# Reordering the two mixing branches of a transformer block: later stick-breaking sums and outputs, decays prepared one pair ahead, output norms moved beside the next pair

## The reference, cut to what matters

```python
h = rms_norm(x, mix_norm_w)
proj = einsum('bsd,de->bse', h, w_in)            # all projections of both branches
# branch 1: stick-breaking attention, 8 heads of 128
q, k = rms_norm(q, sb_q_norm_w), rms_norm(k, sb_k_norm_w)
z = q k^T / sqrt(128);  log_1mb = log_sigmoid(-z) below the diagonal
a = exp(log_sigmoid(z) + suffix_sum(log_1mb));   o_sb = a v
# branch 2: gated delta rule, 8 heads of 128, chunks
gq, gk, gv = silu(conv4(...));  gq, gk = l2_normalize(gq), l2_normalize(gk)
decay = exp(gc_i - gc_j) below the diagonal      # gc: running sum of the log decay
L = strict_lower(k_beta k^T * decay);  T = inverse(I + L)
v_corr = T v_beta;  k_cum = T (k_beta exp(gc));  attn = lower(q k^T * decay)
for chunk in chunks:                             # the recurrence over the state
    v_new = v_corr - k_cum state;  o = q exp(gc) state + attn v_new
    state = state * exp(g_last) + (k exp(g_last - gc))^T v_new
o_gdn = rms_norm(o, gdn_out_norm_w) * silu(z)
x = x + (sigmoid(gate_sb) * (o_sb @ W1) + sigmoid(gate_gdn) * (o_gdn @ W2)) @ w_out
```

## Time and profile before

| | |
|---|---|
| median of 3 runs | 3158.27 us (3157.06 to 3158.77) |
| the profiled execution, its own time | 3154.85 us |
| its span, first to last instruction | 3153.1 us |
| PE busy | 2820.9 us, 89% of the span |
| DVE busy | 1959.8 us, 62% |
| ACT busy | 1168.5 us, 37% |
| POOL busy | 529.7 us, 17% |
| mean granted TensorE clock | 0.95 of full |

### The profile page before, as it was taken

How to read it: one execution, slowest core, us unless ns; L and a number is a source line. 1 busy time by engine, 2 the same in 40 slices (tenths; PEclk the granted TensorE clock), 3 DMA queues, 4 the chain that set the end, 5 groups by cost and what they waited for, 6 DMA issues and landing times.

```text
span 3153.1 us, 36626 instructions
## 1 busy us (share of the span) xinstructions
PE 2820.9 (89%) x14045; PEld 2383.0 (76%) x14045; DVE 1959.8 (62%) x3668; ACT 1168.5 (37%) x1688; POOL 529.7 (17%) x392
## 2 busy tenths in 40 slices
PE   7987798898998799998898799999999878899997
PEld 5666586687776688888898688888888536688876
DVE  3233365465564478989999578787886495354434
ACT  4433433432322333333788222222223344232222
POOL 0111101101000176766211011101110011000000
PEclk9998898899999899998999899999999888999999
DMA  3111111000554256666788788888885200122221
GB/s 135 47 47 47 73 41 41 27 14 28 187 216 165 93 206 249 246 241 235 272 309 321 280 300 293 292 297 295 297 291 183 75 0 28 67 103 91 96 91 40
DMA packets 141357, 501.17 MB, mean 159 GB/s; under 512 B 13400, under 2 KB 66944, under 8 KB 111744
## 3 DMA queue, kind: packets, MB, share of 16 engines
q1 hardware_dynamic: 122752, 364.60, 32.6%
q0 software_dynamic: 18432, 134.23, 10.9%
HBM read 450.53 MB, written 48.25 MB: 158 GB/s over the span
## 4 chain that ended last, share of the span: by engine, by line
PE 63%; DVE 19%; DMA 6%; ACT 5%; issue 3%; POOL 3%; SPq 0%; DVEq 0%; POOLq 0%; ACTq 0%
PE bank L236 17%; PE bank L237 17%; PE bank L238 17%; DMA gs<-in_uv_dram,idx 4%; DVE HA L1823 2%; DVE bank L1491 2%; DVE gs L1478 2%; PE bank L938 1%; PE bank L2395 1%; PE bank L633 1%; PE bank L954 1%; PE bank L948 1%; DVE xn L1289 1%; DVE HO L1820 1%; PE bank L644 1%
## 5 line engine op out<-in xcount | busy, mean ns | idle before, releaser
L236 PE MATMUL bank<-HH,uhl 128*128 128x384 f32 x1024 | 358.8, 350 | 38.5 <-POOL uhl L1413 38.4
L237 PE MATMUL bank<-HL,uhl 128*128 128x384 f32 x1024 | 353.5, 345 | 0.0
L238 PE MATMUL bank<-HH,uhl 128*128 128x384 f32 x1024 | 353.3, 345 | 0.0
L236 PE MATMUL bank<-vhl,awhl 128*128 128x512 f32 x768 | 299.7, 390 | 21.3 <-DVE awhl L2017 21.3
L238 PE MATMUL bank<-vhl,awhl 128*128 128x512 f32 x768 | 299.6, 390 | 0.0
L237 PE MATMUL bank<-vhl,awhl 128*128 128x512 f32 x768 | 299.5, 390 | 0.0
L1467 POOL DMA_INDIRECT gs<-in_uv_dram,idx x128 | 161.4, 1261 | 762.6 <-DVE x L1491 505.3
L1980 ACT ACTIVATE vhl<-vraw 128x1024 fp32r<-128x1024 f32 x128 | 135.8, 1061 | 413.2 <-PE bank L238 272.2
L236 PEld LDWEIGHTS bank<-HH,uhl 128*128 128x128 f32 x1024 | 199.2, 195 | 45.3 <-issue 35.8
L1413 POOL TENSOR_TENSOR uhl<-ur,uhl 128x1024 fp32r<-128x1024 f32 x66 | 159.9, 2429 | 430.3 <-ACT uhl L1407 430.0
L236 PE MATMUL bank<-HH,whl 128*128 128x512 f32 x512 | 212.8, 416 | 18.7 <-DVE whl L232 13.1
(11 more groups left out here) (406 smaller groups left out, 6299.6 us busy)
## 6 DMA issues: line engine op xcount, KB each, us to landing
ur<-in_peer_u_dram SPq DMA_DIRECT2D x128, 512.0 KB
vraw<-in_peer_v_dram SPq DMA_DIRECT2D x128, 512.0 KB, 3.7
w_raw<-in_w_in_dram SPq DMA_DIRECT2D x36, 1024.0 KB, 6.1
xn<-in_ada_rows_dram SPq DMA_DIRECT2D x48, 512.0 KB, 4.7
g_scratch<-stg SPq DMA_DIRECT2D x12, 2048.0 KB, 11.3
gti<-g_scratch SPq DMA_DIRECT2D x16, 1536.0 KB, 9.8
wf_raw<-in_f_w_in_dram SPq DMA_DIRECT2D x22, 1024.0 KB, 4.8
act_scratch<-ag SPq DMA_DIRECT2D x96, 192.0 KB
```

Of the source, the lines that this page charges most:

```text
L236: e.matmul(out, l[0], r[0], start=start, stop=False)
L237: e.matmul(out, l[0], r[1], start=False, stop=False)
L238: return e.matmul(out, l[1], r[0], start=False, stop=stop)
```

## The change

The change writes the lists in another order, and moves buffers so that this is allowed. No matmul and no element-wise product is dropped, except that a [128 x 4] exponential (EGL) is added for each head. Its parts:

- **Start.** Mean square and root are taken row block by row block (`rows_done`). The identity alone is fetched for the transposes, then weights 0, then the other constants. The first weights are split between the third and the fourth tile of HH and HL. PE runs the first two projection steps tile by tile (`pe_sb_first`, `proj_T2`), each as soon as its HL tile is there.
- **Stick-breaking.** The sums move from segment 3 to 4, the exponential to 5, the output matmuls to segment 0 of the next pair (segment 6 for the last). The output copy and its DMA go along.
- **Delta-rule decays.** `pe_decay`, `act_decay`, `dve_decay`, `pool_decay`, `act_decay_exp`, `dve_decay_beta` now run for pair g + 1 within segments 15 to 21 of pair g, and for the first pair within segments 7 to 9 of the last stick-breaking pair.
- **Projection norms.** The squares of the second two tiles get buffers of their own, so all four go together in segments 10 to 12.
- **Output norms.** `pe_gdn_norm`, `act_gdn_norm`, `dve_gdn_norm` run in segments 0 and 1 of the next pair. The output now waits in the XT buffer, so POOL must wait for it before it writes the next XT.
- Explicit loads of the logarithm table on ACT at the head of each pair and in each norm are gone.

```diff
@@ act_norm1, dve_norm1
-        root_x(e, A, V, 0, NT)
-        high_x(e, T, A, R1, lambda kt: vcol("mix_norm_w", kt))
+            if tb:
+                root_x(e, A, V, tb - 1, 1)
+        high_x(e, T, A, R1, lambda kt: vcol("mix_norm_w", kt), range(3))
+        split_hi(e, W, 0)
+        high_x(e, T, A, R1, lambda kt: vcol("mix_norm_w", kt), range(3, KT))
...
@@ pe_sb
+    def pe_sb_first(e):
+        e.wait_ge(*W.low(0).of(0))
+        outs = [R2.take("proj", 0, f)[:, :] for f in range(2)]
...
+        for f, i in enumerate(proj_T2(e, outs, W, 0, wait)):
+            i.then_inc(*T.up("proj", 0, f))
+        W.used(0, T, "proj", 0, 1)
+        pe_sb_norm(e, 0, 0)
...
@@ pe_sb_head: sums along the row
-        if seg == 3:
+        if seg == 4:
@@ pe_sb: outputs
+                if seg == 0 and pair:
+                    for hh in range(2):
+                        pe_sb_out(e, pair - 1, hh)
                 pe_sb_head(e, pair, 0, seg)
                 pe_sb_head(e, pair, 1, seg)
+                if pair == 3 and seg == 6:
+                    for hh in range(2):
+                        pe_sb_out(e, 3, hh)
...
@@ dve_gdn
-            for seg in range(25):
+            for seg in range(24):
                 dve_gdn_head(e, 2 * g, seg)
                 dve_gdn_head(e, 2 * g + 1, seg)
+                if g and seg == 1:
+                    for f in range(2):
+                        dve_gdn_norm(e, 2 * g - 2 + f)
                 if g < 3:
                     dve_gdn_proj(e, R3, g + 1, seg)
+                    for f in range(2):
+                        if seg == 17:
+                            dve_decay(e, R3, 2 * g + 2 + f)
+                        if seg == 21:
+                            dve_decay_beta(e, 2 * g + 2 + f)
...
@@ pe_gdn
+                if g and seg == 0:
+                    for f in range(2):
+                        pe_gdn_norm(e, 2 * g - 2 + f)
                 if g < 3:
                     pe_gdn_proj(e, R3, g + 1, seg)
+                    if seg == 15:
+                        for f in range(2):
+                            pe_decay(e, R3, 2 * g + 2 + f)
@@ pool_gdn_head, seg 1
             e.wait_ge(*A.of("lt", h))
+            if h >= 2:
+                e.wait_ge(*V.of("onw", h - 2))
             e.tensor_tensor(B["XT"][:, :, :], B["LT"][:, :, :], cb("neg1T"), ALU.mult)
```

More of the change, by code:

```diff
@@ L304, in turn_x, with high_x @@
             i.then_inc(*T.up("x", kt))
-    def high_x(e, T, A, R, scale_of):
-        for kt in range(KT):
+    def high_x(e, T, A, R, scale_of, tiles):
+        for kt in tiles:
             e.wait_ge(*T.of("x", kt))
@@ L310, in high_x, with low_x @@
                          scale=scale_of(kt)).then_inc(*A.up("hi", kt))
-    def low_x(e, A, V, R, scale_of):
-        for kt in range(KT):
+    def low_x(e, A, V, R, scale_of, tiles):
+        for kt in tiles:
             e.wait_ge(*A.of("hi", kt))
@@ L803, in pe_sb @@
                     pe_gdn_proj(e, R2, 0, seg)
+                if pair == 3 and seg == 7:
+                    for h in range(2):
+                        pe_decay(e, R2, h)
     def act_sb(e):
@@ L819, in act_sb @@
                     act_gdn_proj(e, R2, 0, seg)
+                if pair == 3 and seg == 7:
+                    for h in range(2):
+                        act_decay(e, R2, h)
+                if pair == 3 and seg == 8:
+                    for h in range(2):
+                        act_decay_exp(e, h)
     def dve_sb(e):
@@ L828, in dve_sb @@
         for pair in range(4):
-            for seg in range(14 if pair == 3 else 6):
+            for seg in range(13 if pair == 3 else 6):
                 dve_sb_head(e, pair, 0, seg)
@@ L837, in dve_sb @@
                     dve_gdn_proj(e, R2, 0, seg)
+                if pair == 3 and seg == 7:
+                    for h in range(2):
+                        dve_decay(e, R2, h)
+                if pair == 3 and seg == 9:
+                    for h in range(2):
+                        dve_decay_beta(e, h)
     def pool_sb(e):
@@ L844, in pool_sb @@
                 pool_sb_head(e, pair, 1, seg)
+        for h in range(2):
+            pool_decay(e, h)
     def sp_sb(e):
@@ L853, in sp_sb @@
         for pair in range(4):
-            for seg in range(14 if pair == 3 else 6):
-                sp_sb_head(e, pair, 0, seg)
-                sp_sb_head(e, pair, 1, seg)
+            for seg in range(13 if pair == 3 else 6):
+                if seg == 0 and pair:
+                    for hh in range(2):
+                        sp_sb_out(e, pair - 1, hh)
+                if pair == 3 and seg == 6:
+                    for hh in range(2):
+                        sp_sb_out(e, 3, hh)
                 if pair < 3:
@@ L885, in pe_gdn_head @@
         if seg == 0:
-            b = R3.take("eg", h)
-            for s in R3.empty("eg", h):
-                e.wait_ge(*s)
-            for tb in range(NT):
-                i = e.matmul(b[:, blk(tb)], gg[:, tb, h:h + 1].broadcast_to([P, P]), const("triu"), start=True,
-                             stop=True)
-            i.then_inc(*T.up("eg", h))
-        if seg == 1:
             b = R3.take("kk", h)
@@ L1159, in pool_gdn @@
                 pool_gdn_head(e, 2 * g + 1, seg)
+            if g < 3:
+                for f in range(2):
+                    pool_decay(e, 2 * g + 2 + f)
     def sp_gdn(e):
```

355 lines of the change are left out of this document (215 added, 140 removed).

## The result

The change made the kernel faster: 3067.7 us median (3058.24 to 3069.71, 4 runs) against 3158.52 (3157.06 to 3161.82, 4 runs), a ratio of 0.9705 with a 95% interval of 0.9684 to 0.9727. That is 91 us, where 104.7 were forecast. The profiled execution took 3058.24 us, its span is 3056.5.

What follows compares the result with a forecast made beforehand. The prediction took TensorE's idle time and half-clock time as the bound. Its terms, 9.0 + 38.8 + 11.5 + 33.6 + 9.0 + 2.8 = 104.7 us, took 3158.27 to 3053.6; own range 3042 to 3068, over the cases 3041 to 3084.

Steps and rivals of the forecast that it cites:

- Start: Kernel start: root per row block and tile-by-tile projection begin TensorE at 19.8 instead of 27.97, at full clock; 9.0 us saved.
- Stick-breaking: Stick-breaking pairs: later sums and outputs remove TensorE's waits for Ls and es and the half clock behind them; 38.8 us saved.
- First boundary: From pair 3's last stick-breaking projection to level 0 of the inverse: 63.8 us becomes 52.3, saving 11.5, bounds 10 and 13.
- the replay: Step-by-step timing of the new order at the boundaries, giving level 0 at 52.3 us in the first, 33.8 in middle ones.
- Second and third boundary: Between delta-rule pairs: VectorE paces, level 0 at 33.8 instead of 55.4 us; 16.8 saved each after decay work, 33.6 together.
- The forecast's sign of being wrong: At the boundaries: the forecast is wrong if VectorE's masks come after 40 us from the boundary.
- VectorE takes the boundary over: Rival, chance 0.14: VectorE has no slack at the boundaries, so they give half, 27 us; time 3081.
- Last boundary: Before the last delta-rule pair, no projections: KW at 11.1, masks at 14.1 us; 9.0 saved, bounds 6 and 11.
- End: End of the mixing stage: copies and squares before norms, no table loads, og near 796.6 instead of 799.4; 2.8 us saved.
- the rival that it stays: Rival, chance 0.11: TensorE's half clock stays in stick-breaking and delta-rule pairs, costing 31 us; time 3085.
- Block behind the merge: Everything from 798 us on: order unchanged and waits on rings, so it moves as a block with its length unchanged.
- three boundaries 45 us longer: Slower rival, chance 0.02: late norms hold KW, VB and XT, each of three boundaries 45 us longer than replayed; 3184.

## Why the prediction was right, and where it was wrong

**Start**: right, to 0.2 us. First matmul forecast at 19.8, seen at 19.65, at full clock; norm matmul 31.9 and 31.74.

**Stick-breaking**: right in the mechanism and near in the sum (38.8 and 41.9, over its bound of 40). What was to be seen was there: no wait for es, 3.1 us for Ls in pair 3. The full clock behind that wait was luck. The forecast left it open at 1.2 us, and of two executions of this kernel one kept the clock and one lost 1.8 us. Its two halves are not additive, as the runs show: outputs alone were costed at 21.2 plus clock and copy and are worth 19.0 at the merge, sums alone 9.9 and 11.2. The waits that the profile lists for a step are not what moving that step is worth while its neighbour stands where it stood.

**First boundary**: near, -11.5 and -10.6. But the decays ahead of the SiLUs lengthen it by 3.5 us (the wait of 10.4 against 6.9); the replay had them in ("ACT free at 6.1") and did not see them as a cost.

**Second and third boundary**: the step that failed. It ran "norms 2.6; convolution 2.8 (0.75 each)", durations from rows where GpSimd stood idle, and gave the overlap with GpSimd no price; the runs show 5.6 us for it and 2.6 of half clock behind. The replay ended at 33.8 us, the trace has level 0 at 41.9 after the last recurrence matmul (458.82 less 416.9, taken 0.4 behind the row's start as the forecast's 475.1 is). The decay work in the recurrence cost 3.5 us (69.9 against 66.4 from level 0 to the last matmul) instead of 4.8. 8.1 less 1.3 is the 6.8 by which -16.8 became -10.0. With GpSimd out of the way the pair takes 7.6 us less, with the norms out of the queue too 9.7. The forecast's sign of being wrong, VectorE's masks after 40 us from the boundary, was at its edge: they ran from 39.1 to 40.4 us.

I had written the cause down as a rival, "VectorE takes the boundary over", with "POOL's XT now waits for the norm" in its favour, and gave it half the boundaries, 27 us. It came true for the middle boundaries and at half that price. What I missed is that a wait on GpSimd's side needs no one waiting for GpSimd to cost: XT was in time, but it moved its traffic onto VectorE's path.

**Last boundary**: forecast 13.8 with the recurrence, 10.7 measured. TensorE's second level-0 product got KW 14.2 us into the boundary (655.63) instead of at 11.1; 1.9 of this is the second head's two norm instructions beside XT (1.75 and 1.56 us). Behind the wait of 5.1 us the clock was 0.50 until 662. **End**: 2.8 and 2.3.

**Half clock**: the rival that it stays was right at the boundaries only: 0.84, 0.87 and 0.89 in the stretches with idle time, 1.00 where TensorE hardly waits, 0.50 for 5.2 us behind the wait of 6.87. The forecast's own 2.0 for it stood at the last boundary alone. The Trainium skill's section "HAM oscillation — how this bites in real kernels", in "TensorE: Matmul & The Clock Gate", cited with that rival, says that such bursts pay at each wait. The rows agree for the waits of 5.1 us and of 6.9 us, each followed by 0.50; they don't for the wait of 3.1 us, which paid in one execution of two, and for 1.26 us, which did not pay.

**Block behind the merge**: held. 91.7 us at the merge and 91 by the medians.

The range, 3041 to 3084, held the time, and the forecast's own 3042 to 3068 held it by 0.3 us. That is partly luck: the middle boundaries gave less than their bound of 12 each, and the stick-breaking part more than its bound of 40. The likeliest time was 14.1 us too low, 13.0 of it by the merge. Two of the forecast's sums are off, without effect on this: its lower bounds add to 82 and not 84, and three boundaries 45 us longer would give 3189 and not 3184.

## What to carry to other kernels

When a wait is moved, look at what the waiting engine will run beside once it is released, not only at who waits for it: here VectorE instructions with two SBUF inputs took twice as long and more beside GpSimd products that read SBUF (0.75 and 1.63 us), and moving two waits on GpSimd's side took that off TensorE's path. An advance preparation was worth something only where nothing covered it (here the last pair), and cost in the place it moved to. And when a change of several moves wins, put each move back alone. Here the start and the stick-breaking moves proved worth 9.6, 11.2 and 19.0 us, while two other named moves cost 6.2 and 11.4. The 38 us of the delta-rule boundaries seem to come from fewer table loads, both copies first and one product a segment sooner, which no run has shown.

## What the hardware showed

- Beside GpSimd's 128x512 products VectorE's two-input instructions took 1.56 to 1.79 us instead of 0.69 to 0.75, most of GpSimd's 1.6 to 1.8 instead of 1.27. One of each in strict turn would take 0.75 + 1.27 = 2.0 us; VectorE's instructions came every 1.5 to 1.9 us there (starts from 437.63 to 445.92), so the two kept each other out for most of their time, not for all. VectorE instructions with PSUM input kept 0.68.
- The convolution's first step, one tensor input in SBUF, went from 0.48 to 1.50 us beside GpSimd.
- Of ten executions with the stick-breaking part unchanged, four kept the clock at 1.00 behind TensorE's wait of 3.1 us and ended the part at 293.4 to 293.6 us. Four had 0.96 from 240 to 280 us and ended it at 294.8 to 295.3. Two had 0.91 from 20 to 40 us as well and ended it at 296.6 and 296.7. Why the same wait brings the clock down in one execution and not in another is open.
